# Second attention: two branches run as one pipeline of sixteen heads

## The reference

```
# branch 1, "forgetting" (heads 0 to 7)
logits = q k^T / 8 + F_t - F_s          # F: running sum of log forget gates
w      = softmax(where(s <= t, logits, -inf));   y = w @ v
# branch 2, "stick breaking" (heads 8 to 15 in the new count)
z      = q k^T / 8
a[t,s] = sigmoid(z[t,s]) * prod_{s<j<t} (1 - sigmoid(z[t,j]))   for s < t, else 0
y      = a @ v                           # written in the reference through log_sigmoid, cumsum, exp
# after both
x += (sigmoid(g1) * (y1 @ W1) + sigmoid(g2) * (y2 @ W2)) @ W_out
```

## Time and profile before

| | us |
|---|---|
| median of 3 runs | 2062.28 (2061.86 to 2062.54) |
| the profiled execution, its own time | 2061.71 |
| its span | 2059.9 |
| PE busy in the span | 2038.7 (99%) |
| ACT / DVE / POOL busy | 734.4 / 883.7 / 1009.8 |

### The profile page before, as it was taken

How to read it: one execution, slowest core, us unless ns; L and a number is a source line. 1 busy time by engine, 2 the same in 40 slices (tenths; PEclk the granted TensorE clock), 3 DMA queues, 4 the chain that set the end, 5 groups by cost and what they waited for, 6 DMA issues and landing times.

```text
span 2059.9 us, 26668 instructions
## 1 busy us (share of the span) xinstructions
PE 2038.7 (99%) x9561; PEld 1670.4 (81%) x9561; DVE 883.7 (43%) x1394; ACT 734.4 (36%) x1006; POOL 1009.8 (49%) x779
## 2 busy tenths in 40 slices
PE   8999999999999999999999999999999999999999
PEld 6798887678888888888888887888778888888887
DVE  6778645534333322153334113577744533332124
ACT  6413224433322223232222224566644422222232
POOL 5345442135555554455555444665544555554543
PEclk9999999999999999999999999999999999999999
DMA  4232322022333332333333232332222333333232
GB/s 159 66 103 83 103 89 74 21 79 85 102 102 100 85 96 93 99 100 102 98 86 97 92 98 82 107 99 72 70 64 82 102 102 98 86 101 97 92 107 82
DMA packets 254153, 188.21 MB, mean 91 GB/s; under 512 B 7552, under 2 KB 249728, under 8 KB 254080
## 3 DMA queue, kind: packets, MB, share of 16 engines
q1 hardware_dynamic: 253392, 186.93, 30.3%
q10 hardware_dynamic: 688, 0.31, 0.1%
HBM read 180.93 MB, written 2.10 MB: 89 GB/s over the span
## 4 chain that ended last, share of the span: by engine, by line
PE 95%; DVE 3%; issue 1%; ACT 1%; DMA 0%; SPq 0%; DVEq 0%; ACTq 0%
PE ps L608 29%; PE ps L610 29%; PE ps L609 29%; DVE sc L1502 1%; PE ps L988 1%; PE ps L829 1%; PE ps L895 1%; PE ps L814 1%; PE ps L897 1%; PE ps L896 1%; PE ps L960 0%; DVE ssum L1630 0%; PE ps L828 0%; PE ps L822 0%; PE ps L1002 0%
## 5 line engine op out<-in xcount | busy, mean ns | idle before, releaser
L500 POOL TENSOR_TENSOR wlo<-raw,whi 128x512 fp32r<-128x512 f32 (+1 forms) x640 | 870.6, 1391 | 923.3 <-ACT whi L1079 916.4
L608 PE MATMUL ps<-xh,whi 128*128 128x512 f32 (+2 forms) x1912 | 735.5, 385 | 9.3 <-DVE xl L1502 7.3
L610 PE MATMUL ps<-xh,wlo 128*128 128x512 f32 (+2 forms) x1912 | 722.1, 378 | 0.0
L609 PE MATMUL ps<-xl,whi 128*128 128x512 f32 (+2 forms) x1912 | 721.8, 378 | 0.0
L1079 ACT ACTIVATE whi<-raw 128x2048 fp32r<-128x2048 f32 (+1 forms) x159 | 297.6, 1871 | 797.8 <-PE ps L610 794.7
L608 PEld LDWEIGHTS ps<-xh,whi 128*128 128x128 f32 (+1 forms) x1912 | 357.9, 187 | 91.7 <-issue 23.9
L610 PEld LDWEIGHTS ps<-xh,wlo 128*128 128x128 f32 (+1 forms) x1912 | 357.7, 187 | 67.9
L609 PEld LDWEIGHTS ps<-xl,whi 128*128 128x128 f32 (+1 forms) x1912 | 358.3, 187 | 64.6 <-issue 2.5
L1556 DVE TENSOR_TENSOR tmp<-ps,rs 128x512 f32<-128x512 f32 x148 | 102.1, 691 | 325.9 <-PE ps L610 308.6
L608 PE MATMUL ps<-fh,whi 128*128 128x512 f32 x528 | 205.4, 389 | 0.0
L609 PE MATMUL ps<-fl,whi 128*128 128x512 f32 x528 | 205.4, 389 | 0.0
(11 more groups left out here) (293 smaller groups left out, 2195.7 us busy)
## 6 DMA issues: line engine op xcount, KB each, us to landing
raw<-in_w_in SPq DMA_DIRECT2D x90, 512.0 KB, 4.6
raw<-in_w_gate_up SPq DMA_DIRECT2D x44, 512.0 KB, 4.7
raw<-in_ffn_w_gate SPq DMA_DIRECT2D x44, 512.0 KB, 3.9
raw<-in_ffn_w_up SPq DMA_DIRECT2D x44, 512.0 KB, 5.1
raw<-in_ffn_w_down SPq DMA_DIRECT2D x32, 512.0 KB, 4.0
raw<-in_w_down SPq DMA_DIRECT2D x16, 512.0 KB, 3.9
raw<-in_ffn_w_down SPq DMA_DIRECT2D x16, 384.0 KB, 3.5
raw<-in_w_b SPq DMA_DIRECT2D x8, 512.0 KB, 4.0
```

What stands on the lines that cost most here:

```text
L500: ins = pool.tensor_tensor(wlo[:, c % 2, cs], raw[:, c % 2, cs], whi[:, c % 2, cs].bitcast(F32), ALU.subtract)
L608: pe.matmul(o, w_of(whi), xhi, start=first, stop=False)
L609: pe.matmul(o, w_of(whi), xlo, start=False, stop=False)
L610: return pe.matmul(o, w_of(wlo), xhi, start=False, stop=last)
```

## The change

Both branches become one list of 16 heads: one list `STEPS` over the 14 chunks, one set of semaphores, the same three-column layout of PSUM banks, two units ahead throughout. The first 40 thirds carry a step each, after that two of three; the last step (67) stands at third 81 of 84, where the last one stood before.

The stick weights are computed as sigmoid(z) times a running product of sigmoid(-z) from the right: two sigmoids on ACT, one scan and one product on DVE. Capping, exp, log, maximum, difference and exp go. The stick values get the two-part layout of the others (`vS` in fp32r, high part by ACT, low part by DVE), the stick probabilities get a low part (DVE), and each of their pieces is two fp32r matmuls into 128 output rows; the two halves are added as for the other branch. POOL makes the low part of all eight pairs. The wait for the outputs is split: `pair` waits for the first four pairs ahead of the loop and for all eight (`second_ready`) ahead of its second half. The sigmoid table is loaded when unit 32, the first stick unit, comes up, instead of behind the stage.

The core of the diff:

```diff
+STEPS, _n = [], 0
+for _third in range(84):
+    _k = 1 if _third < 40 or _third % 3 != 1 and _third < 82 else 0
...
-        vS = at("vS", 16384, [P, QB, T])
+        vS = [at("vS0", 12288, [P, QB, 4, P], F32R), at("vS1", 16384, [P, QB, 4, P], F32R)]
+        rest_of = at("rest_of", 24576, [P, 2, T])
...
 # POOL
-            fox_pair(3)
-            for j in range(8):
...
-                    if third < 3 and j < 7:
-                        low_of_part(c, third)
+            for j in range(14):
...
+                    for n in STEPS[6 * j + third]:
+                        if n % (2 * QB) == QB and n > QB:
+                            pair_low(n // (2 * QB) - 1)
...
+                    if third < 3 and j < 13:
+                        low_of_part(c, third)
+            pair_low(7)
             run(C_MX, C_D[2], 2)
...
 # PE
+                        if z and second_ready is not None:
+                            pe.wait_ge(att["fox"]["y_split"], second_ready)
...
-                pe.matmul(ps[r, 7, P * j:T], vS[:, j, HEAD_DIM * h:HEAD_DIM * h + HEAD_DIM], fpT[h % 2][:, j, P * j:T],
-                          start=j == 0, stop=j == QB - 1).then_inc(B["pv_ready"], 1)
+                pe.matmul(o, v[:, j, :], fpTh[:, j, P * j:T], start=j == 0, stop=False)
+                pe.matmul(o, v[:, j, :], fpTl[:, j, P * j:T], start=False, stop=j == QB - 1).then_inc(F["pv_ready"], 1)
...
-            pe.wait_ge(B["y_split"], 4)
+            pe.wait_ge(F["y_split"], 4)
...
-                    pair(C_MX + q, yfh, yfl, ysh, ysl, 2, i)
+                    pair(C_MX + q, yfh, yfl, ysh, ysl, 2, i, second_ready=8)
...
 # ACT
+            def stick_unit(n):
...
+                act.wait_ge(F["pt_ready"], n - UNITS + 1)
+                act.wait_ge(F["p_ready"], n - 1)
+                act.wait_ge(F["lg_ready"], n + 1)
+                act.activation(pu[:, n % UNITS, 0:w], z, ACT.Sigmoid)
+                act.activation(rest_of[:, n % 2, 0:w], z, ACT.Sigmoid, scale=-1.0).then_inc(F["exp_done"], 1)
...
+                    if n + 2 == QB * HEADS:
+                        act.preload_act_table_set("sigmoid_and_others")
+                    stick_unit(n + 2)
...
+            pair_high(7)
             high(C_MX + 1)
...
 # DVE
+            def stick_share(n):
...
+                link(dve.tensor_tensor_scan(rest[:, ::-1], rest[:, ::-1], rest[:, ::-1], 1.0, ALU.mult, ALU.bypass))
+                dve.tensor_tensor(p, p, rest[:, 1:w], ALU.mult).then_inc(F["p_ready"], 1)
```

More of the change, by code:

```diff
@@ L50 @@
 UNITS = 4
-Z_TOP = 60.0
 TAKEN = -3.0e38
@@ L69 @@
     0, 8, 16, 24, 32, 40, 48, 56, 80, 84, 96, 97, 98, 99, 99)
[L73 to L76, removed]
+STEPS, _n = [], 0
+for _third in range(84):
+    _k = 1 if _third < 40 or _third % 3 != 1 and _third < 82 else 0
+    STEPS.append(range(_n, _n + _k))
     _n += _k
+PAIRED = 2 * HEADS
+SCORED = PAIRED * QB
 DSA_STEPS = {6 + n * 54 // (QB * HEADS + QB - 1): n for n in range(QB * HEADS + QB)}
@@ L306, in out_bank, with values_of, outputs_of @@
             return 7 - h % 2
[L308 to L312, removed]
+        def values_of(h):
+            return vF[:, :, h, :] if h < HEADS else vS[(h - HEADS) // 4][:, :, h % 4, :]
+        def outputs_of(i):
+            return (yfh[:, i, :], yfl[:, i, :]) if i < 4 else (ysh[:, i - 4, :], ysl[:, i - 4, :])
         def near(h):
@@ L325, in stacked_at @@
         def stacked_at(n):
-            return (n + 6) // QB if n % QB == 2 and n + 6 < QB * HEADS else None
+            return (n + 6) // QB if n % QB == 2 and n + 6 < SCORED else None
         kin = "(k p) n -> p k n"
@@ L437, in _ @@
             second(2)
-            for j in range(6):
+            for j in range(11):
                 for third in range(6):
-                    if stacked_at(6 * j + third) is not None:
-                        doubled(F, stacked_at(6 * j + third), kt1, qt1, qt2)
+                    for n in STEPS[6 * j + third]:
+                        h = stacked_at(n)
+                        if h is not None and h < HEADS:
+                            doubled(F, h, kt1, qt1, qt2)
+                        elif h is not None:
+                            doubled(B, h - HEADS, sk1)
                     if third == 3:
                         second(j + 3)
[L444 to L452, removed]
             wf = I["w_branch_fox_2"][0].rearrange(kin, p=P)
@@ L565, in _, with pair_low @@
             pool.wait_ge(st_zero, 2)
-            def fox_pair(i):
+            def pair_low(i):
+                hi, lo = outputs_of(i)
                 pool.wait_ge(F["hi_done"], i + 1)
-                pool.tensor_tensor(yfl[:, i, :], ysum, yfh[:, i, :].bitcast(F32), ALU.subtract).then_inc(F["y_split"], 1)
+                pool.tensor_tensor(lo, ysum, hi.bitcast(F32), ALU.subtract).then_inc(F["y_split"], 1)
                 pool.wait_ge(F["y_split"], i + 1)
@@ L665, in norm_sums, with pair @@
                 mm.then_inc(ss_done, 1)
-            def pair(c, hi_a, lo_a, hi_b, lo_b, per, i):
+            def pair(c, hi_a, lo_a, hi_b, lo_b, per, i, second_ready=None):
                 s = c % 2
@@ L962, in fox_step @@
                 if h >= 1:
[L963 to L987, removed]
-                pe.matmul(ps[r, 7, P * j:T], vS[:, j, HEAD_DIM * h:HEAD_DIM * h + HEAD_DIM], fpT[h % 2][:, j, P * j:T],
-                          start=j == 0, stop=j == QB - 1).then_inc(B["pv_ready"], 1)
[L991 to L1005, removed]
+                    value_piece(h - 1, q)
             pe.wait_ge(hq_rt, 8)
@@ L1009, in _ @@
             pe.wait_ge(f_lo, 2)
-            fox_qk(0)
-            fox_qk(1)
-            for j in range(6):
+            scores(0)
+            scores(1)
+            for j in range(14):
                 c = C_SQ + j
@@ L1016, in run @@
                     if k in THIRDS:
[L1017 to L1025, removed]
-                    chunk(c, xh, xl, steps=run)
[L1027 to L1036, removed]
-            pe.wait_ge(B["y_split"], 4)
+                        for n in STEPS[6 * j + 3 * t + THIRDS.index(k)]:
+                            second_step(n)
+                if C_SV <= c < C_GF:
+                    tokens(c, steps=run)
+                else:
+                    chunk(c, xh, xl, steps=run)
+            pe.wait_ge(F["y_split"], 4)
             with pe.Fori(0, 2) as i:
                 for q in range(2):
-                    pair(C_MX + q, yfh, yfl, ysh, ysl, 2, i)
+                    pair(C_MX + q, yfh, yfl, ysh, ysl, 2, i, second_ready=8)
             with pe.Fori(0, 2) as i:
@@ L1364, in _ @@
             act.wait_ge(rtok_done, 1)
-            values_high(C_FV, 0)
-            values_high(C_FV + 1, 1)
+            for j in range(2):
+                for t in range(2):
+                    values_high(C_FV + j, t, vF, 4 * j)
             def high_part(c, part):
@@ L1449, in _ @@
-                    if j == 5 and 2 <= third < 5:
-                        softplus(third - 2)
-                        if third > 2:
-                            sb_unit(third - 3)
-            fox_pair(3)
-            for j in range(8):
-                for third in range(6):
-                    for n in SB_STEPS[6 * j + third]:
-                        sb_step(n)
-                    if third < 3:
-                        high_part(C_GF + j + 1, third)
+                        high_part(c + 1, third)
```

235 lines of the change are left out of this document (88 added, 147 removed).

## The result

The changed kernel takes 2055.58 us (median of 7 runs, 2054.2 to 2056.89) against 2061.86 us (7 runs, 2061.66 to 2062.54): ratio 0.9968, 95% interval 0.9957 to 0.9979. It is faster by 6.3 us, 0.3%. I had said 2050.5 us with a range up to 2054.5, so the time lies 1.1 us above the range; the sum had a gain of 11.8 us. The profiled execution's own time is 2055.58 us, its span 2053.4.

A forecast was written before the change was run, and what follows sets the result against it. PE was taken as the bound. Pieces 18.0 us less, seam 0.7 and end of the stage 5.5 us more: 11.8 us less, from the profiled 2061.71 to 2049.9, median 2050.5 us; range 2047.0 to 2054.5.

The forecast's parts named there:

- The clock: Rival, behind PE's long idle wait: PE restarts slowly at 1.2 GHz, costing 1.7 us, so 2052.2 us; chance 0.27.
- the seam: Switch from forgetting to stick heads: table load and unit chain make PE wait, 0.7 us more, bounds 0 and 2.5.
- What bounds the kernel: Whole kernel: PE is busy 99% of the span, so gains come only from PE's work or its waits.
- The value pieces: Stick heads' value matmuls become like forgetting heads': 2.25 us a head, 8 heads, 18.0 us less; bounds 17 and 18.5.
- Edits costed at nothing: Work moved on ACT, DVE, POOL and SP was said to cost nothing as long as PE covers it.
- The end of the stage: Before C_MX: PE waits because POOL makes the last pair's low part before low(C_MX); 5.5 us more, bounds 5.0 and 6.1.
- The stick chain: Rival, steps 30 to 39: PE waits each step; mild 2053 (chance 0.10), through all units 2066 (0.04 including other new waits).
- POOL's order costs nothing: Rival, end of stage: low(C_MX) is done in time anyway, the 5.5 us stay with the gain, 2045.0 us; chance 0.07.
- the pieces were not the cost: Rival, stick value pieces: a split piece costs as much as the float32 one, leaving two waits, 2068.5 us; chance 0.02.

## Why the prediction was wrong

Three terms make the miss. The clock behind the long wait stood at nothing in the sum and cost 2.8 us; POOL's order within a chunk stood at nothing and cost 1.65 us; the seam stood at 0.7 us and cost 2.1. The pieces gave 0.8 us more than the sum had, and the long wait was 0.25 shorter: 4.8 us less gain in all than the 11.8 forecast.

**What bounds the kernel: right.** PE is the bound, and every microsecond of the result is work or a wait of PE.

**The value pieces, 18.0 us: the size right, the cause half wrong.** The stage of the run without a table load is 236.76 - 217.99 = 18.8 us shorter than before, so 18.0 was sound, though 18.8 lies 0.3 us above my upper bound of 18.5. It came out right because it was taken from whole heads and not from the sum over one kind of matmul. But the text named plain float32 and the 128 output rows together and never asked for the share of each. Given in stages: 10.2 us are the 64-column form and 5.2 us the float32 passes, each with what they cover of waits; 3.7 us (221.73 - 217.99) are waits that show beside fast pieces, and 0.4 go off because the run with 64-column pieces is that much longer than the kernel before. That the slower pieces had covered the 3.7 us is argued: PE had no wait here before the change. That I did not know the shares cost me the forecast of the plain-piece run by 10 us.

**Edits costed at nothing: here one step failed.** I wrote that SP's, ACT's and POOL's new order costs nothing as long as PE covers it, and looked at busy shares. Nothing in the sum asked on which third the stacking of a head falls once four steps make a chunk. It falls ahead of the last `wlo` part in five chunks, and this is 1.65 us by the stage, in no term of mine. "Short of time" was not POOL, busy 50% of the span; its queue was in the wrong order.

**The seam, 0.7 us: mis-sized.** It measured 2.1 us, inside the bounds of 0 to 2.5. The place (the copy of unit 31 behind the load) and the 4.3 us were right. The first wait measured 0.3 us where I had 0.4; for all that follows I had another 0.3, and it was 1.8, because the lateness is handed on. The chain with a product at 1.29 us and a scan beside POOL's work has no slack in the dense stretch. The value taken should have been near the upper bound, since the row that is nearest to the product was L1581, and I took L1995: 0.69 us is what the old difference cost, and the product costs as little only where POOL is idle. The rule of the Trainium skill on the shared pair of ports (SBUF — State Buffer, "SBUF: two separate sides") agrees with this trace: 0.42 us for a product of 255 columns with POOL idle, 0.77 us and more beside POOL's subtractions.

**The end of the stage, 5.5 us: right.** It is 5.25 us, by the mechanism and the place named, and the order alone removes it. Its terms were 3.56, 0.23, 5.08 and 3.62 us for my 3.7, 0.1, 5.2 and 3.4.

**The clock: the rival that came true, and with a larger price.** I gave it 0.27, at 1.7 us. It cost 2.8 us in the profile and 2.7 between medians. The price was the step that failed there: I took it from the kernel's start, where 3.4 us had passed at the low level, and took half of them. Behind the wait the low level lasted 5.7 us, and half of it is 2.8. The rule of the Trainium skill (TensorE: Matmul & The Clock Gate, "Part 1: The HAM clock gate"), that an idle PE drops to 1.2 GHz, agrees with this trace: 0.43 us for 512 columns. With a mechanism whose condition I had myself written into the sum (a wait of 5.5 us, in a trace whose longest later gap was 1.4), the case without it was not the likelier one. One reading there was loose: the 0.33 us behind the gap of 1.41 us is the first start alone and lies between the two levels; that the clock had not fallen is shown by the starts after it, at 22.49, 22.73 and 22.95 us.

So 2050.5 becomes: 18.8 - 2.1 - 1.65 - 5.25 - 2.8 = 7.0 us less for the span, against 6.5 measured; what is left, 0.5 us, holds the 0.1 of the start; the terms come from different executions, and the rest is not settled.

**The other rivals.** The stick chain cost 2.1 us in all and kept up once two steps took three thirds (its sum was 2066.5, where the text has 2066). "POOL's order costs nothing" and "the pieces were not the cost" fell.

## What to carry to other kernels

When work moves into one shared list, write out the queue of each engine for one period of the new list, and look at what now stands ahead of the item that the bounding engine waits for; the share of busy time says nothing about that. A wait of the matrix engine has to be priced twice when it is long, once for itself and once for the clock behind it. And take the price of a matmul from its neighbours' starts too: an operand of 64 columns costs the matmul behind it as well.

## What the runs showed of the hardware

- A stationary operand of 64 columns among ones of 128: 0.14 us more for a float32 piece of 512 columns (1.00 against 0.86) and 0.19 us more for the matmul behind it (0.43 against 0.24), with the weight loads of both starting no earlier than their matmuls.
- After 5.25 us without work PE's next 13 matmuls of 512 columns started 0.43 us apart, which is 1.2 GHz; with the same gap filled by 22 matmuls nobody reads they started 0.23 us apart.
- A DVE product of two SBUF tiles of 127 columns took 0.91 us in the mean, 0.91 to 1.21 beside POOL's subtractions and 0.29 the one time that POOL was idle; a difference of 128 columns with one side in PSUM took 0.29. With POOL idle products of 255 and 383 columns took 0.42 and 0.56 us; beside POOL they took 0.77 us at least.
